# Two activation buffers of a fourteen-stage transformer kernel at another SBUF address

## The reference

```python
def swiglu(h, w_gu, w_down):
    g, u = jnp.split(h @ w_gu, 2, axis=-1)
    return (jax.nn.silu(g) * u) @ w_down

for layer in range(DEPTH):                       # first block
    x = x + 0.5 * swiglu_ffn(rms_norm(x, ffn1_norm[layer]), ffn1_w_gu[layer], ffn1_w_down[layer])
    h = rms_norm(x, mix_norm[layer])
    x = x + even_mixer(h, ...)                   # odd_mixer in layer 1
    x = x + memory_cross_attention(rms_norm(x, xa_norm[layer]), rms_norm(mem, xa_mem_norm[layer]), ...)
    x = x + 0.5 * swiglu_ffn(rms_norm(x, ffn2_norm[layer]), ffn2_w_gu[layer], ffn2_w_down[layer])
for l in range(DEPTH):                           # second block
    x = x + FFN_SCALE * rmsnorm(swiglu(rmsnorm(x, ffn1_norm_pre[l]), ffn1_w_gu[l], ffn1_w_down[l]), ffn1_norm_post[l])
    x = x + rmsnorm(mixer(rmsnorm(x, mix_norm_pre[l])), mix_norm_post[l])
    x = x + FFN_SCALE * rmsnorm(swiglu(rmsnorm(x, ffn2_norm_pre[l]), ffn2_w_gu[l], ffn2_w_down[l]), ffn2_norm_post[l])
```

## Time and profile before

| | |
|---|---|
| runs | 2721.49, 2722.61, 2722.82 us |
| the profiled execution's own time | 2721.7 us |
| its span, first to last instruction | 2719.6 us |
| mean granted clock of TensorE | 0.987 of full speed |
| TensorE matmuls | 2642.8 us busy, 97% of the span, 18604 of them |
| VectorE | 1922.2 us, 71% |
| ScalarE | 1503.1 us, 55% |
| GpSimd | 198.2 us, 7% |
| weight stream | 829 loads of 512 KB, 3.3 us from issue to landing |

### The profile page before, as it was taken

One profiled execution on the slowest core, in us unless ns is written; L12 is line 12 of the kernel. 1 busy time (PEld: TensorE's weight loads), 2 busy tenths in 40 slices (PEclk: granted clock), 3 DMA queues, 4 the chain that ended last, 5 costly groups with the idle time before them and its releaser, 6 DMA issues.

```text
span 2719.6 us, 51716 instructions
## 1 busy us (share of the span) xinstructions
PE 2642.8 (97%) x18604; PEld 2438.3 (90%) x18604; DVE 1922.2 (71%) x3131; ACT 1503.1 (55%) x2579; POOL 198.2 (7%) x280
## 2 busy tenths in 40 slices
PE   8999799999999999999999999999999999999998
PEld 7998699999998899999998998989989999988997
DVE  7776676778777575777777667777777776676875
ACT  6556556556555656556555555655565555555554
POOL 0001001000000201000000160000000005200000
PEclk9999899999999999999999999999999999999999
DMA  7554234655554344555654542445545545335553
GB/s 260 201 185 135 83 132 149 223 201 184 186 185 155 101 156 133 186 186 168 201 185 141 177 156 94 162 155 185 185 156 185 186 146 164 124 113 167 170 186 108
DMA packets 122821, 445.80 MB, mean 164 GB/s; under 512 B 13688, under 2 KB 14712, under 8 KB 122688
## 3 DMA queue, kind: packets, MB, share of 16 engines
q1 hardware_dynamic: 120816, 436.79, 48.7%
q0 software_dynamic: 1872, 7.17, 0.7%
HBM read 442.86 MB, written 1.05 MB: 163 GB/s over the span
## 4 chain that ended last, share of the span: by engine, by line
PE 94%; DVE 4%; ACT 1%; issue 0%; DMA 0%; SPq 0%; DVEq 0%; ACTq 0%
PE bank L454 93%; PE bank L805 1%; DVE rt L1696 1%; DVE z L1534 0%; DVE w_lo L1468 0%; DVE rt L1490 0%; DVE x L1527 0%; DMA x<-in_x_dram 0%; DVE a L1495 0%; ACT w_hi L1034 0%; ACT score L1268 0%; ACT L1242 0%; DVE z L1702 0%; DVE z L1824 0%; DVE z L1827 0%
## 5 line engine op out<-in xcount | busy, mean ns | idle before, releaser
L454 PE MATMUL bank<-a,w_hi 128*128 128x256 f32 (+1 forms) x5360 | 1353.2, 331 | 37.9 <-DVE a L1495 37.6
L1468 DVE TENSOR_TENSOR w_lo<-raw,w_hi 128x1024 fp32r<-128x1024 f32 x829 | 1017.1, 1231 | 282.2 <-ACT w_hi L1034 281.3
L454 PEld LDWEIGHTS bank<-a,w_hi 128*128 128x128 f32 x5360 | 904.6, 192 | 126.6 <-issue 45.1
L454 PE MATMUL bank<-a,w_lo 128*128 128x256 f32 x3736 | 1017.2, 283 | 0.0
L1034 ACT CAST w_hi<-raw 128x1024 fp32r<-128x1024 f32 x829 | 857.8, 1046 | 44.1 <-DMA raw<-in_stream_dram 34.1
L454 PE MATMUL bank<-b,w_hi 128*128 128x256 f32 (+1 forms) x4096 | 871.5, 304 | 3.5 <-DVE b L1495 2.5
L454 PEld LDWEIGHTS bank<-a,w_lo 128*128 128x128 f32 x3736 | 715.3, 191 | 16.5
L454 PEld LDWEIGHTS bank<-b,w_hi 128*128 128x128 f32 x4096 | 664.9, 190 | 40.7 <-issue 3.6
L454 PE MATMUL bank<-b,w_lo 128*128 128x256 f32 x2400 | 664.0, 282 | 0.0
L454 PEld LDWEIGHTS bank<-b,w_lo 128*128 128x128 f32 x2400 | 455.6, 190 | 5.6
L1081 ACT COPY pt<-bank 128x256 f32<-128x256 f32 x176 | 65.6, 372 | 219.8 <-PE bank L454 219.8
(11 more groups left out here) (185 smaller groups left out, 2132.3 us busy)
## 6 DMA issues: line engine op xcount, KB each, us to landing
raw<-in_stream_dram SPq DMA_DIRECT2D x829, 512.0 KB, 3.3
z<-in_biasc_dram POOLq DMA_DIRECT2D x6, 512.0 KB, 4.5
z<-in_biasa_dram POOLq DMA_DIRECT2D x3, 512.0 KB, 4.4
x<-in_x_dram SPq DMA_DIRECT2D x2, 512.0 KB, 7.7
v<-in_mem_dram POOLq DMA_DIRECT2D x2, 512.0 KB, 6.7
out_dram<-x SPq DMA_DIRECT2D x8, 128.0 KB, 1.9
con<-in_con_dram POOLq DMA_DIRECT2D x1, 912.0 KB, 6.8
vec<-in_vec_dram POOLq DMA_DIRECT2D x1, 417.0 KB, 5.6
```

The costliest lines, as they stand in the source:

```text
L454: return nc.tensor.matmul(out, lhsT, rhs, start=start, stop=stop, skip_group_check=shared)
L1468: return nc.vector.tensor_tensor(out, a, hi.bitcast(F32), ALU.subtract)
```

## The change

The line that makes `a` and `b`, with the four views of their halves, moves from ahead of `z` to behind `hmid`. Shapes, formats, the order of all instructions and all waits stay as they are.

```diff
         x = sb("x", [P, C, T])
-        a_two, b_two = sb("a", [P, C, 2, T], F32R), sb("b", [P, C, 2, T], F32R)
-        a_hi, a_lo = a_two[:, :, 0, :], a_two[:, :, 1, :]
-        b_hi, b_lo = b_two[:, :, 0, :], b_two[:, :, 1, :]
         z = sb("z", [P, 49, T])
...
         sil = sb("sil", [P, 2, T])
         hmid = sb("hmid", [P, 2, T])
+        a_two, b_two = sb("a", [P, C, 2, T], F32R), sb("b", [P, C, 2, T], F32R)
+        a_hi, a_lo = a_two[:, :, 0, :], a_two[:, :, 1, :]
+        b_hi, b_lo = b_two[:, :, 0, :], b_two[:, :, 1, :]
         vec = sb("vec", [P, NVEC])
```

## The result

The changed kernel takes 2694.85 us (median of five runs, 2694.39 to 2696.44), beside 2722.68 us of the kernel before in the same rounds: a ratio of 0.9899, with a 95% interval of 0.9885 to 0.9913. It is 27.8 us or 1.0% faster, where no difference was forecast. The profiled execution's own time is 2694.85 us and its span 2692.8 us, 26.8 us shorter than before; the mean granted clock is 0.987 in both.

A forecast was written before the change was run, and what follows sets the result against it. The prediction took TensorE's matmul pace, with waits at stage starts, to bound the kernel. Three terms of 0 summed to 0, with 0.8 us either way, leaving a median of 2722.6 us, range 2719.5 to 2725.5.

The forecast's parts named there:

- The bound of the kernel: Whole span: TensorE has a matmul under way in 97%, and line 454's helper makes 93% of the chain that ended last.
- the first term, 0 x 17,080: Matmuls on `a` and `b`: their new address changes nothing in 17,080 of 18,604 matmuls; value 0, bounded at 0.4 us.
- the exchange of `a` and `b`: Feed-forward stages 2 and 4: buffers swap roles, 16 KiB apart, and steps 3 to 20 take 144.27 us in both.
- values against the rest: Where values are made, weights move and `a` or `b` is loaded: median 283 ns, as with `a` moving.
- The fp32 matmuls at 379 ns: Plain fp32 matmuls on `v`, `score`, `sil`: 379 ns at three addresses, taken as nearest rows for the region above 104 KiB.
- its open end: Above 104 KiB no fp32r matmul reads before the change; a price there would make the prediction wrong.
- The second and third term: Writes of `a` and `b`: 0, at most 0.4 us either way; temporaries lying 32 KiB lower: 0.
- the wait: TensorE's waits at line 1495, for the normed input's low part: forecast to stay near 37.6 us.
- The slower rivals: Two cases of a slower kernel, beside the temporaries 0.03 and by alignment 0.02, together 0.05.
- The one beside the temporaries: Feed-forward steps: matmul reads held up by VectorE's and ScalarE's neighbouring accesses; 21 us slower, 2744 us; chance 0.03.
- one by alignment: Rival: the kernel gets slower by the alignment of the moved buffers; chance 0.02.
- The chance of a faster kernel: Rival: the change makes the kernel faster instead of leaving its time the same; chance 0.04.

## Why the prediction was wrong

**The bound of the kernel was right.** TensorE's pace in line 454 sets the end. The arithmetic that a price on an operand of `a` or `b` is paid 17,080 times with nothing to hide it was right too: the gain of 27.8 us is 1.6 ns for each. It should have been the warning.

**The step that failed is the first term, 0 x 17,080.** It was bounded at 0.4 us either way, and the 64 bytes gave 27.8 us. It rested on places where "the trace before already varies the address": the exchange of `a` and `b`, and values against the rest. These vary the region. They don't vary the difference, which was 0 for each of them, since 16 KiB is a multiple of 256 bytes. So 144.27 us against 144.27 us was a comparison of a case with itself, and the bound of 0.4 us drawn from it bounds only what it varied. The fp32 matmuls at 379 ns didn't help either. That they keep 379 ns after the change says nothing: `v`, `score` and `sil` moved by 32 KiB exactly and `con` not at all, so their difference within 256 bytes stayed. In the kernel with the new place and the difference undone, `sil` and `hmid` lie 64 bytes lower still against `con`, and their matmuls keep their 379 ns (tile view of `con`):

```profile
L454 PE MATMUL bank<-hmid,con x54: 377/379/483, 215.7 to 1029.5; 128*128 128x256 f32 x32, 128*32 128x256 f32 x22
L454 PE MATMUL bank<-sil,con x52: 377/379/634, 219.3 to 1022.4; 128*128 128x256 f32 x32, 128*32 128x256 f32 x20
```

So at 64 bytes this form doesn't respond, and rows of it could not stand in for fp32r.

**What the prediction named as its open end** was an fp32r operand above 104 KiB. That was the wrong open end: with the difference at 0, the new region takes 2721.75 us.

**The second and third term were right.** The cast stayed at 406 ns into both buffers, line 1495 at 477, the fp32 matmuls at 379, the wait at 38.6 beside 37.6 us. The slower rivals didn't come true. The one beside the temporaries would have shown in the kernel with the new place and the difference undone, which takes the 144.27 us of before. The 0.02 for one by alignment was my estimate: no row and no run shows a unit in which TensorE fetches. What the runs showed is that moving operands and weights together by 64 bytes was worth nothing (144.27 us), and that at 8 bytes the steps are longer than at 0 (145.07 beside 144.27 us).

**The chance of a faster kernel was far too small.** I put it at 0.04, because the pace is the same for `a` and for `b`, and with the roles of weights and activations exchanged. That speaks of regions, and region was the wrong measure of how close two operands lie; what counts is the place within 256 bytes. No run shows the shortest step that a matmul of 256 columns can take, so 0.04 was my estimate. What the runs showed is 0.12 us from start to start before and 0.113 at 16 bytes, where 49 us were had, on an engine with nothing beside it.

**What is shown and what is open.** Shown: the gain comes from the difference of the operands' addresses within 256 bytes, at every place tried; region, neighbours, the whole layout's alignment and the ring's writers have no part in it. Not shown is what inside the chip it is. That the pattern repeats after 256 bytes rests on one pair, 0 and 256. The value at each difference can't be derived from what was run, and rings at separate differences don't add up. Differences between 128 and 240 bytes were not tried, so not 64 bytes with the other sign either.

## What to carry to other kernels

Where TensorE sets the end, shift the buffer of one operand against the other by 16 to 64 bytes and measure; here a view that starts 16 bytes later was worth 1.8% and cost no instruction. A layout of round sizes gives every pair of operands the same difference, 0, which here was among the slowest. And before a trace's own variation is taken as evidence that something doesn't matter, write down which digits of it vary.

## What the runs showed of the hardware

- The pace of fp32r matmuls depends on the difference of the addresses of the operand sent through and the operand loaded: 17 steps took 140.47 us at 16 bytes, 144.27 at 0 and at 256, 144.39 at 96 and 145.07 at 8. Plain fp32 matmuls of `sil` and `hmid` by `con` kept their 379 ns when their difference changed by 64 bytes.
- It isn't smooth: 16, 32, 48 and 64 bytes give ratios of 0.9822, 0.9876, 0.9944 and about 0.990. 16 ahead and 16 behind differ (0.9822 and 0.9894).
- The best difference depends on the form: at 64 bytes the value tiles, weights sent through, are at 276 ns and the product down at 280, beside 283 and 283 before; at 16 they are at 281 and 276; at 8 bytes the value tiles gain (278) and the feed-forward steps lose.
- Taking away nearly all of the ring's other traffic, 1600 us of ScalarE's and VectorE's work, left the steps at 144.27 us.
